# The second feed-forward takes both parts of h in one matmul of 512 columns, and the modulation steps beside it are moved

## The reference, cut to what matters

```
mod = c_act @ w_mod[i] + b_mod[i]                 # six vectors of 1024: shift, scale, gate for each half
h = modulate(rmsnorm(x, g_mix_pre[i]), sh_a, sc_a)
...                                               # attention
x = x + gt_a * rmsnorm(o, g_mix_post[i])
h = modulate(rmsnorm(x, g_ffn_pre[i]), sh_f, sc_f)
gate = h @ w_ffn_gate[i]                          # 256 x 2816
up = h @ w_ffn_up[i]
gate = causal_depthwise_conv(gate, w_conv[i], b_conv[i])   # 3 taps along the tokens
y = (silu(gate) * up) @ w_ffn_down[i]
x = x + gt_f * rmsnorm(y, g_ffn_post[i])
```

## Time and profile before

| | us |
|---|---|
| median of three runs (1361.14 to 1364.23) | 1362.74 |
| profiled execution | 1363.81 |
| its span | 1362.5 |
| its layer 1 gate and up products, 488.15 to 617.04 | 128.9 |
| its layer 1 down product with the first transposes behind it, 617.04 to 679.40 | 62.4 |
| its layer 2 gate and up products, 883.49 to 1007.31 | 123.8 |

### The profile page before, as it was taken

How to read it: one execution, slowest core, us unless ns; L and a number is a source line. 1 busy time by engine, 2 the same in 40 slices (tenths; PEclk the granted TensorE clock), 3 DMA queues, 4 the chain that set the end, 5 groups by cost and what they waited for, 6 DMA issues and landing times.

```text
span 1362.5 us, 20647 instructions
## 1 busy us (share of the span) xinstructions
PE 1298.8 (95%) x8024; PEld 1135.3 (83%) x8024; DVE 1079.2 (79%) x1691; ACT 770.0 (57%) x1330; POOL 45.2 (3%) x74
## 2 busy tenths in 40 slices
PE   4999899999999889999989999899999899999998
PEld 3998799998798689998777786688888799788887
DVE  6887788887868788779887886798887887777753
ACT  4755745553856575554574666765543644655541
POOL 0022000000014100000000000000000000000000
PEclk8999899999999999999999999999999999899999
DMA  9966587679577544667934433167788576347550
GB/s 375 374 233 226 184 300 280 265 292 375 187 297 280 187 158 171 253 249 267 354 124 155 171 121 127 63 267 306 292 297 342 211 285 255 126 184 292 225 203 37
DMA packets 46738, 319.96 MB, mean 235 GB/s; under 512 B 5216, under 2 KB 5808, under 8 KB 9648
## 3 DMA queue, kind: packets, MB, share of 16 engines
q1 hardware_dynamic: 46640, 318.63, 61.7%
HBM read 317.51 MB, written 1.10 MB: 234 GB/s over the span
## 4 chain that ended last, share of the span: by engine, by line
PE 65%; DVE 17%; DMA 7%; ACT 6%; issue 4%; SPq 0%; POOL 0%; ACTq 0%; DVEq 0%
PE mat L663 10%; DVE wlo L1724 7%; PE mat L736 7%; PE mat L738 6%; PE mat L740 6%; PE mat L698 5%; PE mat L662 5%; PE mat L700 5%; PE mat L699 5%; DVE raw L1751 3%; ACT whi L1217 3%; DMA raw<-in_down 2%; DMA raw<-in_mod 2%; PE mat L1106 2%; PE mat L1108 2%
## 5 line engine op out<-in xcount | busy, mean ns | idle before, releaser
L1724 DVE TENSOR_TENSOR wlo<-raw,whi 128x1024 fp32r<-128x1024 f32 x393 | 475.8, 1223 | 140.5 <-ACT whi L1217 137.6
L1217 ACT ACTIVATE whi<-raw 128x1024 fp32r<-128x1024 f32 x393 | 406.1, 1052 | 195.8 <-DMA raw<-in_down 75.3
L698 PE MATMUL mat<-hHL,whi 128*128 128x256 f32 x1080 | 308.4, 286 | 3.9 <-DVE tmp L2271 2.8
L699 PE MATMUL mat<-hHL,whi 128*128 128x256 f32 x1080 | 305.5, 283 | 0.0
L700 PE MATMUL mat<-hHL,wlo 128*128 128x256 f32 x1080 | 305.5, 283 | 0.0
L1751 DVE SCALAR_TENSOR_TENSOR raw<-raw,cB 128x1024 f32<-128x1024 f32 x180 | 218.1, 1222 | 12.6 <-DMA raw<-in_mod 12.3
L663 PE MATMUL mat<-hHL,whi 128*128 128x512 f32 x616 | 221.4, 399 | 0.0
L698 PEld LDWEIGHTS mat<-hHL,whi 128*128 128x128 f32 x1080 | 207.1, 192 | 8.9 <-DVE tmp L2271 4.3
L699 PEld LDWEIGHTS mat<-hHL,whi 128*128 128x128 f32 x1080 | 207.1, 192 | 0.1
L700 PEld LDWEIGHTS mat<-hHL,wlo 128*128 128x128 f32 x1080 | 207.1, 192 | 0.0
L662 PE MATMUL mat<-hHL,wlo 128*128 128x256 f32 x616 | 172.8, 281 | 0.0
(11 more groups left out here) (237 smaller groups left out, 1872.8 us busy)
## 6 DMA issues: line engine op xcount, KB each, us to landing
raw<-in_mod SPq DMA_DIRECT2D x89, 1024.0 KB, 5.6
raw<-in_qkv SPq DMA_DIRECT2D x46, 1024.0 KB, 6.9
raw<-in_gate SPq DMA_DIRECT2D x44, 1024.0 KB, 5.2
raw<-in_up SPq DMA_DIRECT2D x44, 1024.0 KB, 4.9
raw<-in_down SPq DMA_DIRECT2D x44, 1024.0 KB, 5.9
raw<-in_wo SPq DMA_DIRECT2D x16, 1024.0 KB, 5.0
begin<-in_mod SPq DMA_DIRECT2D x6, 1024.0 KB, 17.0
gtb<-gates SPq DMA_DIRECT2D x8, 512.0 KB, 7.1
```

Of the source, the lines that this page charges most:

```text
L698: pe.matmul(o, wh[:, k, :], hH[:, k, :], start=(k == 0), stop=False)
L699: pe.matmul(o, wh[:, k, :], hL[:, k, :], start=False, stop=False)
L1217: act.activation(whi[:, n % NSPL, :], raw[:, f % NRAW, 1024 * h:1024 * h + 1024], ACT.Copy).then_inc(s_hi, 1)
L1724: dve.tensor_tensor(out=wlo[:, n % NSPL, :], in0=raw[:, f % NRAW, 1024 * h:1024 * h + 1024], in1=whi[:, n % NSPL, :].bitcast(f32), op=ALU. ...
```

## The change

`PARTED` takes in layer 1, so that its 22 pairs of gate and up halves are made by `parted_product`, with the boundary's first pair by `parted_boundary`. The gate sum now goes back into the SBUF tile of the second column range (`gate_low`), and the bias, the three taps and the SiLU read from there instead of from PSUM. ACT and DVE call `hi` and `lo` one at a time between these steps where there were two.

Two of the eight steps of vector (2, 1) move from the feed-forward of layer 1 into its attention (head steps 8 and 9), the steps of (1, 5) move one head step back, and the other six of (2, 1) stand behind `lo` of the halves 4, 11, 18, 25, 32 and 39 of the feed-forward (before: all eight, behind 8, 12, 17, 22, 27, 31, 36 and 41). Gate (1, 5) is turned and copied after the up products instead of at the boundary, and its way through DRAM moves from the gate chunks 7 and 9 to the down chunks 7 and 9.

```diff
--- before.py
+++ after.py
@@ -133,8 +133,10 @@
     _spread([(0, 4)], heads(0, 13, 17))
     _spread([(0, 5), (1, 1), (1, 0)], halves(START["ffn", 0] + 4, START["ffn", 0] + 46))
     _spread([(1, 2), (1, 3)], halves(START["ffn", 0] + 46, START["ffn", 0] + 66))
-    _spread([(1, 4), (1, 5)], heads(1, 0, 16))
-    _spread([(2, 1)], halves(START["ffn", 1] + 8, START["ffn", 1] + 46))
+    _spread([(1, 4)], heads(1, 0, 8))
+    _spread([(2, 1)], heads(1, 8, 10), 0, 2)
+    _spread([(1, 5)], heads(1, 9, 18))
+    _spread([(2, 1)], halves(START["ffn", 1] + 4, START["ffn", 1] + 46), 2)
     _spread([(2, 0), (2, 2)], halves(START["ffn", 1] + 46, START["ffn", 1] + 64))
     _spread([(2, 3)], heads(2, 6, 10))
     _spread([(2, 4)], heads(2, 16, 19))
@@ -184,7 +186,7 @@
 def _gate_loads():
     for gate, after, then in (
             ((0, 2), ("wo", 0, 6), ("gate", 0, 0, 0)), ((0, 5), ("down", 0, 14), ("down", 0, 18)),
-            ((1, 2), ("q", 1, 3, 0), ("k", 1, 3, 0)), ((1, 5), ("gate", 1, 7, 0), ("gate", 1, 9, 0)),
+            ((1, 2), ("q", 1, 3, 0), ("k", 1, 3, 0)), ((1, 5), ("down", 1, 14), ("down", 1, 18)),
             ((2, 2), ("d", 4, 0, 0), ("d", 5, 0, 0)), ((2, 5), ("down", 2, 14), ("down", 2, 18)),
             ((3, 2), ("c", 2, 0), ("c", 3, 0)), ((3, 5), ("down", 3, 16), ("down", 3, 20))):
         GATE_OUT["w", CHUNK_OF[HALF[after]][0]] = gate
@@ -367,7 +369,7 @@
 
         BY_TILE = (2, 4)
 
-        PARTED = (2, 3)
+        PARTED = (1, 2, 3)
         PARTED_BANKS = (5, 0, 2)
 
         def parted_bank(j, up):
@@ -760,8 +762,6 @@
         def tensor_boundary(b):
             transposes(b, 0, 0, 1)
             transposes(b, 0, 2, 3)
-            if b == 3:
-                gate_row(1, 5)
             if b == 6:
                 gate_row(3, 2)
             for p in range(2):
@@ -862,8 +862,7 @@
                     if k == 0 and l in PARTED:
                         pe.wait_ge(s_gsum if t else s_usum, parted_count(l, 10 if t else 9) + 1)
 
-                if l != 1:
-                    gate_row(l, 5)
+                gate_row(l, 5)
                 token_product(range(HALF["down", l, 0], HALF["down", l, 0] + FT), FT, token_order(FT, [1] * 9 + [2], 1 if l < 2 else 2), aH, aL, a_ready)
                 if l < 2:
                     by_tile_begin(2 * l + 2)
@@ -1308,8 +1307,6 @@
             for p in (2, 3):
                 scalar_pair(b, 1, p)
                 scalar_high(b, 1, p)
-            if b == 3:
-                gate_taken(1, 5)
             if b == 6:
                 gate_taken(3, 2)
             hi(4)
@@ -1391,8 +1388,7 @@
                 scalar_ffn(l)
                 if l < 3:
                     act.preload_act_table_set("natural_log_exp_and_others")
-                if l != 1:
-                    gate_taken(l, 5)
+                gate_taken(l, 5)
                 if l == 1:
                     hi(6)
                     act.wait_ge(s_ctx, 16)
@@ -1671,11 +1667,23 @@
             i, y = parted_count(l, j), tmp[:, j % 3, :]
             if i >= 2:
                 act.wait_ge(s_gsum, i - 1)
+            if l < 2 and j >= 2:
+                act.wait_ge(s_gconv, 2 * (11 * l + j - 1))
             act.activation(gate_low(j), low_part(parted_bank(j, 0)), ACT.Copy).then_inc(s_glow, 1)
             hi(1)
             act.wait_ge(s_gsum, i + 1)
+            if l < 2:
+                if j >= 3:
+                    act.wait_ge(s_al, 11 * l + j - 2)
+                for n in range(2):
+                    bias, w2 = (sm[:, SM[name][0] + 2 * j + n:SM[name][0] + 2 * j + n + 1] for name in (f"bc{l}", f"wc{l}2"))
+                    m = act.activation(y[:, 256 * n:256 * n + 256], gate_low(j)[:, n], ACT.Identity, bias=bias, scale=w2)
+                m.then_inc(s_gate, 1)
+                hi(1)
+                act.wait_ge(s_gconv, 2 * (11 * l + j) + 2)
             act.activation(y, y, ACT.Silu).then_inc(s_silu, 1)
-            hi(1)
+            if l >= 2:
+                hi(1)
             act.wait_ge(s_half, HALF["up", l, j, 1] + 1)
             if i >= 2:
                 act.wait_ge(s_mul, 11 * l + j - 1)
@@ -2260,7 +2268,18 @@
             for j in range(11):
                 y, g = two(tmp[:, j % 3, :]), two(bank(4))
                 lo(1)
+                if l in PARTED:
+                    i = parted_count(l, j)
+                    dve.wait_ge(s_glow, i + 1)
+                    if j >= 3 and l >= 2:
+                        dve.wait_ge(s_al, 11 * l + j - 2)
+                    dve.tensor_tensor(out=gate_low(j) if l < 2 else y, in0=high_part(parted_bank(j, 0)), in1=gate_low(j),
+                                      op=ALU.add).then_inc(s_gsum, 1)
+                    lo(1)
                 if l < 2:
+                    if l in PARTED:
+                        g = gate_low(j)
+                        dve.wait_ge(s_gsum, i + 1)
                     dve.wait_ge(s_gate, 11 * l + j + 1)
                     for back in (1, 0):
                         w = [sm[:, SM[f"wc{l}{back}"][0] + 2 * j + n:SM[f"wc{l}{back}"][0] + 2 * j + n + 1] for n in range(2)]
@@ -2271,13 +2290,7 @@
                             m = dve.scalar_tensor_tensor(out=y[:, n, at:256], in0=g[:, n, 0:256 - at], scalar=w[n],
                                                          in1=y[:, n, at:256], op0=ALU.mult, op1=ALU.add)
                         m.then_inc(s_gconv, 1)
-                else:
-                    i = parted_count(l, j)
-                    dve.wait_ge(s_glow, i + 1)
-                    if j >= 3:
-                        dve.wait_ge(s_al, 11 * l + j - 2)
-                    dve.tensor_tensor(out=y, in0=high_part(parted_bank(j, 0)), in1=gate_low(j), op=ALU.add).then_inc(s_gsum, 1)
-                lo(2)
+                lo(1 if l in PARTED else 2)
                 if l in PARTED:
                     u = up_low(j)
                     dve.wait_ge(s_ulow, i + 1)
```

## The result

The changed kernel took 1369.49 us (median of six runs, 1364.6 to 1374.2), the kernel before in the same comparison 1362.49 (1361.1 to 1365.9). The ratio is 1.0054, with a 95% interval of 1.0035 to 1.0072: it is slower by 7.0 us. I had forecast 2.3 us slower on the median, so the sign was right and the size was a third of what came. The median lies at the very end of my range (1358.4 to 1369.5). The profiled execution has a span of 1370.3 us, 7.8 more than before.

The account below looks back on a forecast made before the run. DVE's program up to low half 54 was taken to bound layer 1's feed-forward. DVE 0.4, attention 1.75 and gate 0.3 make 2.4 us on the median 1362.7: 1365.1, rounded to 1365.0, range 1358.4 to 1369.5.

Parts of the forecast that it names:

- rival 2: Layer 1's gate and up products: refills take 6 us or more instead of 4.8; 1368.6 to 1374.6 us; chance 0.22.
- The bound: Layer 1's feed-forward is set by DVE's program up to low half 54, where PE's 5.1 us gain is paid back.
- The refills: Layer 1's gate and up products: weight chunks wait for buffers held by modulation steps, three DVE holes, 13.7 us together.
- rival 1: Layer 1's feed-forward: refills cost nothing and PE is the bound, 4.2 us faster, 1358.5; chance 0.20.
- DVE's way to half 54: Layer 1, first gate matmul to low half 54: DVE needs 156.4 us, 0.4 later than before.
- of each step I leave 0.15 for the up sum behind ACT's copy: Layer 1's gate and up products: DVE's waits for ACT mostly go, 1.6 us in all remain.
- The attention: Layer 1's attention: the steps at head steps 8 and 9 outlast DVE's idle time and delay PE by 1.75 us.
- Rival 3: Layer 1's attention hides its two steps, 1.75 us less, 1363.3; chance 0.08.
- The gate: Layer 1's down product: the gate's 512 KB read, moved there, costs 0.3 us, between 0 and 1.6.
- behind half 54 all is as before: Layer 1's down product after half 54 stays unchanged; no further delay was counted there.
- The taps from SBUF: Layer 1's tap instructions take the same time from SBUF as from PSUM; counted as 0.
- rival 4: Layer 1's tap instructions get cheaper from SBUF by the skill page's figures, 2.8 us less, 1362.2; chance 0.08.

Follow-up runs that it names:

- e2: Changed kernel with layer 1's six feed-forward steps of (2,1) in three adjacent pairs, behind low halves 6, 7, 18, 19, 30, 31; 1359.6 us.
- e3: Changed kernel with gate (1,5) turned behind the second up product and written and read at gate chunks 7 and 9 as before; 1369.9 us.
- e5: Kernel before with only the changed plan of modulation steps in layer 1's attention and feed-forward, old 256-column form; 1379.8 us.
- e10: Changed kernel loading only 256 of 2048 columns of the (2,2) modulation chunks, so that vector is not computed; 1367.8 us.
- e8: e7 with gate (1,5) also written and read at gate chunks 7 and 9 as before; 1356.1 us.
- e12: e7 loading only 256 of 2048 columns of the (2,2) modulation chunks, so that vector is not computed; 1354.3 us.
- e13: e7 with the (2,0) and (2,2) steps spread to place 70 instead of 64, two modulation chunks asked for later, nothing left out; 1354.9 us.
- e7: Changed kernel with all eight (2,1) steps in layer 1's feed-forward in four adjacent pairs, and the attention's old plan; 1356.6 us.

## Why the prediction was right in its direction and wrong in its size

**The forecast as a whole.** I summed 0.4 + 1.75 + 0.3 us. The same three terms came out as 2.4, 2.5 and 2.2. All three were too small, so the direction did not hang on one of them; but that the time still lies inside the range is luck. The upper end of the range stood there for rival 2, longer refills, and that is not what happened.

**The bound.** Right: what PE saves in the gate and up products waits at low half 54. PE's stage was 126.5 us, not my 124 to 125, since the last of the refills already shows in it (1.4 us at 609.53) and the clock was low for the first 4 us (0.50, then 0.73).

**The refills.** Right, and the heart of the change: three waits of 13.35 us in all where I had 13.7, and ACT began each time 4.8 to 5.0 us after an issue that came with a modulation step. e2 places the same six steps so that these waits go, and gains 9.4. It also places four of the steps 2 to 8 halves earlier and one 2 later; no run has the early places with long holds, but DVE's work before half 54 is the same in both, so I put the gain down to the waits. Rivals 1 and 2 fall; rival 1 gave what the kernel would do without them (1358.5), and e2, without them, took 1359.6.

**DVE's way to half 54.** This is the first step that failed, 2.0 of the 4.7 us that I missed: "of each step I leave 0.15 for the up sum behind ACT's copy". The new sums are followed by instructions that wait for ACT or for the sum itself. DVE's timeline of one step:

```profile
613.59 1.22 DVE L1732 TENSOR_TENSOR wlo<-raw,whi 128x1024 fp32r<-128x1024 f32 x1
614.91 1.79 DVE L2290 SCALAR_TENSOR_TENSOR tmp<-tmp,sm 128x255 f32<-128x255 f32 x4
616.62 1.22 DVE L1732 TENSOR_TENSOR wlo<-raw,whi 128x1024 fp32r<-128x1024 f32 x1
617.89 0.69 DVE L2297 TENSOR_TENSOR tmp<-mat,tmp 128x512 f32<-128x512 f32 x1
618.61 0.69 DVE L2303 TENSOR_TENSOR tmp<-tmp 128x512 f32<-128x512 f32 x1
619.22 1.22 DVE L1732 TENSOR_TENSOR wlo<-raw,whi 128x1024 fp32r<-128x1024 f32 x1
```

A low half is followed after 1.32 us by the taps and after 1.27 by the up sum, where I counted 1.14, and the sum is followed after 0.72 by the product that reads it, where I counted 0.61. The first two waits are absent where a modulation step or a refill stands in between, the third is in all eleven steps. Added up over DVE's timeline that is 1.5 for the taps, 1.2 for the up sum (0.45 of it in the first step) and 1.2 for the product, 3.9 us in all against my 1.6. With it my sum becomes 137.5 + 3.5 + 3.9 + 13.35 = 158.2, and low half 54 began 158.4 us after the first gate matmul, not 156.4. The stops before half 54 were 6 us, as forecast, but I had placed them all at 50 to 54: half of it is the bank in half 44, a wait that I had not followed.

**The attention.** Forecast 1.75, measured 2.5 in this trace. The cover was right: both idle pieces of DVE are gone in the changed kernel, and PE's wait for head 9 ends 2.5 us later. What I had at nothing is that DVE's instructions take longer there. Two pieces of DVE's timeline in the changed kernel, and what POOL does beside them:

```profile
439.14 1.30 DVE L1759 SCALAR_TENSOR_TENSOR raw<-raw,cB 128x1024 f32<-128x1024 f32 x1
440.37 1.41 DVE L1732 TENSOR_TENSOR wlo<-raw,whi 128x1024 fp32r<-128x1024 f32 x1
...
439.33 1.38 POOL L2367 TENSOR_SCALAR_AFFINE_SELECT att<-tmp 128x256 f32<-128x256 f32 x1
```

These DVE instructions take 1.22 us elsewhere, and POOL's select 0.40 where no large DVE instruction runs beside it. Before, it was so once in this stretch (440.07), in the changed kernel three times (439.33, 444.58, 450.64). From start to start that is 0.8 us more on DVE than before, which with 3.4 of steps less some 1.7 of idle pieces gives the 2.5. Nothing was run to test it by itself. The four other kernels with these steps there (e2, e3, e5, e10) have the same 2.5 up to head 9's transposes; over the whole way they have 92.9, 92.6, 92.4 and 91.9, and the trace of e2 shows why they differ: around and behind the stop of 3.6 us its clock was 0.74, 0.50 and 0.56, where the changed kernel had 0.84, 0.62 and 1.00. Rival 3 falls.

**The gate, and "behind half 54 all is as before".** Both failed, and this is the second large step, 1.9 of the 4.7 us. I charged 0.3 for the gate's read; measured is 2.2 more between half 54 and 65. e3 shows that it is not the read, and so does e8, which without the read at this place still stops for 1.5 us before half 63. The traces of e10 and e12 show that it goes with the bytes: with 3.5 MB less to load it is gone. This stretch already ran near its transfers' limit before, and does so in the changed kernel (in the columns of the earlier trace rows, first two rows before, then changed):

```profile
645.00:662.00 17.00, 16.56 (x73) 13.71 (x74) 16.50 (x22) 6.04 (x6) 0.00 (x0) 1.00 0.95 376
662.00:680.00 18.00, 17.67 (x79) 13.67 (x77) 14.27 (x20) 12.45 (x23) 0.00 (x0) 1.00 0.93 365
...
654.00:672.00 18.00, 17.92 (x79) 14.86 (x80) 16.31 (x23) 6.03 (x6) 0.00 (x0) 1.00 0.95 369
672.00:690.00 18.00, 15.79 (x67) 11.79 (x65) 13.71 (x18) 11.71 (x22) 0.00 (x0) 1.00 0.95 371
```

The share is what to go by, not the rate: e10's last 18 us (666 to 684) show 0.98 and 406 GB/s. In the prediction I had read the share of the whole down product (0.83) and not that of its last 35 us, which have no room for a down product that has to catch up. How much of it comes in one execution varies: layer 0's down product, with the same kind of load, took between 59.7 and 63.7 us in these traces.

**The taps from SBUF.** As taken: 481 ns against 475 before (changed, then before).

```profile
L2290 DVE SCALAR_TENSOR_TENSOR tmp<-tmp,sm 128x255 f32<-128x255 f32 x20 | 8.8, 481 | 0.8
...
L2271 DVE SCALAR_TENSOR_TENSOR tmp<-mat,sm,tmp 128x255 f32<-128x255 f32 x22 | 9.5, 475 | 0.0
```

The saving that the Trainium skill's figures would give ("VectorE: DVE Perf Modes", section "The TRN2 errata") is not there, and rival 4 falls.

**What stays open.** The account of 7.1 us rests on one execution of each kernel for its three parts. That e10 gained only 0.8 us of median where its trace gained 3 behind half 54 is not explained. e12 and e13 point the same way as its trace, but neither is told from e7 by its interval. The small waits of DVE and POOL's part in the attention are read from traces and not tested by a run of their own.

## What to carry to other kernels

A buffer's place in a ring is paid for by the time it is held: two steps that share a loaded chunk belong next to each other, and the chunk that comes into the buffer after them should be due later than a transfer's 5 us. Before hiding work on an engine "that has room", ask how far it stands ahead at the next hand-over, and price every pair of instructions that depend on each other across engines. Read the DMA share of the last stretch of a stage, not of its mean: time won on the engines ahead of a stretch that runs at the transfers' limit is given back in it.

## What the runs showed of the hardware

A stop of PE can cost more than its length. After the stop of 3.3 us that ended at 616.5 in e5 the granted clock was 0.50, 0.50 and 0.62 in three stretches of 2 us, then 1.00:

```profile
616.50:618.50 2.00, 1.98 (x9) 1.98 (x10) 1.08 (x2) 2.00 (x3) 0.00 (x0) 0.50 1.03 434
618.50:620.50 2.00, 2.00 (x11) 2.00 (x11) 2.00 (x3) 2.00 (x4) 0.00 (x0) 0.50 0.78 246
620.50:622.50 2.00, 2.00 (x13) 2.00 (x12) 1.96 (x5) 0.68 (x2) 0.00 (x0) 0.62 0.74 295
622.50:624.50 2.00, 2.00 (x19) 2.00 (x18) 1.48 (x2) 1.28 (x2) 0.00 (x0) 1.00 0.70 229
```

Counted in matmuls it is 33 in 6 us where the pace of the earlier trace rows (24 in 2.88 us) would give 50, so 2 us are lost on top of the stop's 3.3. It is not the same each time: after the stop of 2.73 us at 625.22 in the changed kernel the clock stayed at 1.00, and after the same stop in e10 it was 0.50 for 6 us.

DVE and POOL can slow each other. In the attention POOL's select of 128x256 took 1.38 us beside a DVE instruction of 128x1024 and 0.40 where no such instruction ran, and the DVE instruction 1.30 or 1.41 instead of 1.22.
